# A fused two-block kernel on one core: the first norm by column halves, gate units as two matmuls per k tile, channel sums on VectorE, a masked quarter left out, and one convolution tile on GpSimd

## The reference, cut to what matters

```python
def _even_layer(x, norm_g, w_in, b_glu, w_dw, b_dw, ln_g, ln_b, w_pw, b_pw, w_out):
    z = _rmsnorm(x, norm_g) @ w_in                       # 2048 -> 7 x 1024
    a_val, a_gt, a_gate, q, k, v, b_gate = _split_cols(z, [1024] * 7)
    ya = _conformer_conv(a_val + b_glu[:1024], a_gt + b_glu[1024:],
                         w_dw, b_dw, ln_g, ln_b, w_pw, b_pw) * jax.nn.silu(a_gate)
    ...                                                  # causal attention of 8 heads on q, k, v: yb
    ...                                                  # yb * silu(b_gate), and both through w_out

def _conformer_conv(a_val, a_gt, w_dw, b_dw, ln_g, ln_b, w_pw, b_pw):
    u = a_val * jax.nn.sigmoid(a_gt)
    y = lax.conv_general_dilated(u, w_dw[:, None, :], window_strides=(1,), padding=[(30, 0)],
                                 feature_group_count=1024) + b_dw     # 31 taps per channel
    y = jax.nn.silu(_layernorm(y, ln_g, ln_b))                        # over the 1024 channels
    return y @ w_pw + b_pw
```

## Time and profile before

| | us |
|---|---|
| three runs: median (lowest to highest) | 2568.4 (2568.16 to 2569.23) |
| the profiled execution | 2565.47 |
| its span, first to last instruction | 2563.7 |
| PE busy | 2486.2 (97%) |
| DVE busy | 1622.7 (63%) |
| ACT busy | 1176.6 (46%) |
| POOL busy | 151.1 (6%) |

### The profile page before, as it was taken

The page is one execution under the profiler, slowest core; times in us unless marked ns, Lnnn a source line. Parts: engine busy times, 40 slices in busy tenths (PEclk is TensorE's granted clock), DMA queues, the critical chain, the costliest instruction groups (busy, mean ns, idle before and its releaser), DMA issues.

```text
span 2563.7 us, 35901 instructions
## 1 busy us (share of the span) xinstructions
PE 2486.2 (97%) x14366; PEld 2175.2 (85%) x14366; DVE 1622.7 (63%) x1941; ACT 1176.6 (46%) x1371; POOL 151.1 (6%) x136
## 2 busy tenths in 40 slices
PE   6999999999889999999999999999999999999998
PEld 6888998898778788988888888888888888888886
DVE  4799755545674776486565545445677557755764
ACT  5433754444464554542345444334655334433333
POOL 0000000000200100000000000000022001210220
PEclk9999999999999999999999999999999999999999
DMA  7565436554424555554026555535455555655553
GB/s 236 165 197 189 142 131 229 150 165 133 144 83 159 157 185 172 170 164 132 1 82 214 187 180 192 164 132 184 160 182 196 192 183 183 196 187 185 186 174 138
DMA packets 341284, 422.91 MB, mean 165 GB/s; under 512 B 14491, under 2 KB 267178, under 8 KB 340394
## 3 DMA queue, kind: packets, MB, share of 16 engines
q1 hardware_dynamic: 338620, 411.66, 49.1%
q0 software_dynamic: 2160, 8.40, 1.0%
q10 hardware_dynamic: 382, 1.11, 0.1%
HBM read 419.05 MB, written 2.10 MB: 164 GB/s over the span
## 4 chain that ended last, share of the span: by engine, by line
PE 94%; DVE 4%; ACT 2%; issue 0%; DMA 0%; ACTq 0%; DVEq 0%
PE ps L678 29%; PE ps L679 15%; PE ps L723 9%; PE ps L725 9%; PE ps L724 9%; PE ps L681 4%; PE ps L682 4%; PE ps L683 4%; PE ps L944 3%; PE ps L754 1%; DVE w_lo L1844 1%; PE ps L912 1%; PE ps L885 1%; PE ps L1141 1%; PE ps L1132 1%; PE ps L901 0%
## 5 line engine op out<-in xcount | busy, mean ns | idle before, releaser
L678 PE MATMUL ps<-h_cat,w_hi 128*128 128x512 f32 x3200 | 1137.0, 400 | 8.2 <-DVE qo L1877 8.0
L679 PE MATMUL ps<-h_cat,w_lo 128*128 128x256 f32 x3200 | 897.7, 281 | 0.0
L1844 DVE TENSOR_TENSOR w_lo<-ring,w_hi 128x2048 fp32r<-128x2048 f32 (+2 forms) x282 | 592.3, 2102 | 278.6 <-ACT w_hi L1221 275.6
L678 PEld LDWEIGHTS ps<-h_cat,w_hi 128*128 128x128 f32 x3200 | 602.2, 188 | 159.1 <-DVE w_lo L1844 6.1
L679 PEld LDWEIGHTS ps<-h_cat,w_lo 128*128 128x128 f32 x3200 | 605.5, 189 | 2.1 <-issue 1.9
L1221 ACT ACTIVATE w_hi<-ring 128x2048 fp32r<-128x2048 f32 (+2 forms) x282 | 495.8, 1759 | 98.9 <-PE ps L725 84.5
L1840 DVE TENSOR_TENSOR w_lo<-ring,w_hi 128x2048 fp32r<-128x2048 f32 (+1 forms) x136 | 303.1, 2232 | 232.0 <-ACT w_hi L1218 231.9
L1218 ACT ACTIVATE w_hi<-ring 128x2048 fp32r<-128x2048 f32 (+1 forms) x136 | 252.7, 1862 | 285.4 <-PE ps L725 263.4
L723 PE MATMUL ps<-w_hi,h_cat 128*128 128x512 f32 x704 | 275.9, 392 | 4.7 <-DVE h_cat L2013 3.0
L725 PE MATMUL ps<-w_hi,h_cat 128*128 128x512 f32 x704 | 274.7, 390 | 0.0
L724 PE MATMUL ps<-w_lo,h_cat 128*128 128x512 f32 x704 | 274.7, 390 | 0.0
(11 more groups left out here) (380 smaller groups left out, 2460.0 us busy)
## 6 DMA issues: line engine op xcount, KB each, us to landing
ring<-in_w_ffn_up SPq DMA_DIRECT2D x44, 2048.0 KB, 8.0
ring<-in_even_w_in SPq DMA_DIRECT2D x28, 2048.0 KB, 8.1
ring<-in_w_mix_in SPq DMA_DIRECT2D x28, 2048.0 KB, 8.3
ring<-in_w_ffn_down SPq DMA_DIRECT2D x16, 2048.0 KB, 8.0
ring<-in_odd_w_in SPq DMA_DIRECT2D x11, 2048.0 KB, 8.3
ring<-in_even_w_out SPq DMA_DIRECT2D x8, 2048.0 KB, 8.1
ring<-in_odd_w_out SPq DMA_DIRECT2D x8, 2048.0 KB, 8.1
ring<-in_w_mix_out SPq DMA_DIRECT2D x8, 2048.0 KB, 8.1
```

What stands on the lines that cost most here:

```text
L678: mm(o[:, 0:2 * T], whi[slot][:, k, :], flat(cat[:, k]), start=first, stop=False)
L679: ins = mm(o[:, T:2 * T], wlo[slot][:, k, :], cat[:, k, 0, :], start=False, stop=end)
L1844: tt(wlo[slot][:, 0:g.kt, 0:m], chunk(c % RING, g)[:, :, u0:u0 + m], whi[slot][:, 0:g.kt, 0:m].bitcast(F32), ALU.subtract).then_inc(sem["l ...
```

## The change

Five things change, with the orders that follow from them.

1. First norm. x comes in four transfers (two token halves by two column halves), each with its own semaphore; ACT squares four quarters; the row of the norm's gain comes first and is turned and copied by itself; POOL loads the other eleven rows and makes `w_hi` of unit 0 in two casts; DVE makes its `w_lo` in two halves between pieces of `h_cat`.
2. Gate units. The segments e_gt, e_bgate, e_agate, o_gate0, o_gate1 and g_z (48 units) become paired: ACT copies, DVE adds, and a further ACT instruction applies sigmoid or silu in place (`gate_function`), with a new semaphore `gated`.
3. Channel sums. DVE sums 8 tiles into one (`channel_sum`), and PE multiplies that one by ones, at u = 10 and u = 12. The centring on DVE moves from step 14 to step 13.
4. Masked quarter. Scores of the first 128 queries against the last 128 keys are not made, nor the transpose of that quarter; DVE clears that part of banks 2 and 3 once, at the start of e_bgate.
5. Tile 0 of the convolution goes to POOL as 31 multiplies and 31 adds of 128x256. DVE keeps 217 taps, in groups of tiles (1, 2), (3, 4), (5, 6, 7): 6 or 7 per unit from e_val's sixth on, 7 in e_v, and 8, 8, 8, 7 in e_bgate.

```diff
+        self.gated = name in ("e_gt", "e_bgate", "e_agate", "o_gate0", "o_gate1", "g_z")
-        self.paired = staged or name in ("e_k", "e_q", "o_iq", "o_q", "g_c", "x_q", "x_k")
+        self.paired = staged or self.gated or name in ("e_k", "e_q", "o_iq", "o_q", "g_c", "x_q", "x_k")
...
     @block.sync
-        sp.dma_start(x[:, 0, :], a["x"][0, 0:P]).then_inc(sem["x_loaded0"], 16)
+        for h in range(2):
+            cols = slice(h * D // 2, (h + 1) * D // 2)
+            sp.dma_start(x[:, 0, cols], a["x"][0, 0:P, cols]).then_inc(sem[f"x_loaded0{h}"], 16)
...
     GpSimd
+        for row in first_table[1:]:
+            load_rows(pool, row, "params_loaded")
+        pool.wait_ge(sem["first_loaded"], 16)
+        for half in range(2):
+            k = slice(8 * half, 8 * half + 8)
+            pool.tensor_copy(whi[0][:, k, :], chunk(0, order[0])[:, k, 0:P]).then_inc(sem["first_hi"], 1)
...
+        pool.wait_ge(sem["params_ready"], 3)
+        pool.wait_ge(sem["posted"], S["e_val"].s0 + 1)
+        for tap in range(TAPS):
+            w = prm[:, COL["dw"] + tap * CT:COL["dw"] + tap * CT + 1]
+            if tap:
+                pool.wait_ge(sem["pool_tap"], 2 * tap)
+            pool.tensor_tensor(xsq[:], u[:, 0, tap:tap + T], w.to_broadcast([P, T]), ALU.mult).then_inc(sem["pool_tap"], 1)
+            pool.wait_ge(sem["pool_tap"], 2 * tap + 1)
+            before = conv[:, 0, :] if tap else prm[:, COL["b_dw"]:COL["b_dw"] + 1].to_broadcast([P, T])
+            pool.tensor_tensor(conv[:, 0, :], xsq[:], before, ALU.add).then_inc(sem["pool_tap"], 1)
...
     @block.tensor: e_scores, the transposes, beside e_bgate and e_agate
             for qt in range(TT):
-                ins = mm(o[:, qt * T:(qt + 1) * T], qe[:, h, qt * P:(qt + 1) * P], ke[:, h, :], start=True, stop=True)
+                keys = (qt + 1) * P
+                ins = mm(o[:, qt * T:qt * T + keys], qe[:, h, qt * P:(qt + 1) * P], ke[:, h, 0:keys], start=True, stop=True)
...
-                for qt in range(TT):
+                for qt in range(kt, TT):
...
                 if u_ == 1:
-                    pe.wait_ge(sem["emptied"], 4)
+                    pe.wait_ge(sem["quarter_clear"], 1)
...
-                if u_ == 11:
-                    pe.wait_ge(sem["conv_tap"], TAPS * CT)
+                if u_ == 10:
+                    pe.wait_ge(sem["conv_total"], 1)
+                    pe.wait_ge(sem["masked"], HEADS - 1)
+                    mm(ps[2][:, 0:T], ones[:], xsq[:], start=True, stop=True).then_inc(sem["conv_mean"], 1)
+                if u_ == 12:
+                    pe.wait_ge(sem["conv_total"], 2)
                     pe.wait_ge(sem["masked"], HEADS)
-                    for c in range(CT):
-                        ins = mm(ps[2][:, 0:T], ones[:], conv[:, c, :], start=(c == 0), stop=(c == CT - 1))
-                    ins.then_inc(sem["conv_mean"], 1)
...
+                    mm(ps[3][:, 0:T], ones[:], xsq[:], start=True, stop=True).then_inc(sem["conv_var"], 1)
...
     @block.scalar: drain
-            if g.staged:
+            if g.gated:
+                if g.name == "e_bgate":
+                    act.wait_ge(sem["pool_tap"], 2 * TAPS)
+                    if j >= 1:
+                        act.wait_ge(sem["conv_tap"], taps_through(j))
+                ins = af(gated_tile(g, jj), src, ACT.Copy)
+            elif g.staged:
...
+        def gate_function(g, j, i=None):
+            jj = j if i is None else j + 4 * i
+            act.wait_ge(sem["summed"], g.d0 + jj + 1)
+            v = gated_tile(g, jj)
+            if g.name == "e_gt":
+                ins = af(v, v, ACT.Sigmoid, bias=col("b_glu", CT + jj))
+            else:
+                ins = af(v, v, ACT.Silu)
+            ins.then_inc(sem["gated"], 1)
...
     @block.vector
+        def channel_sum(tiles):
+            nc.vector.tensor_reduce(xsq[:], tiles[:].rearrange("p c t -> p t c"), AX_X, ALU.add).then_inc(sem["conv_total"], 1)
...
-            taps = conv_taps(204, 11)
+            taps = conv_taps(186, 8)
...
+                if u_ == 0:
+                    dve.wait_ge(sem["emptied"], 4)
+                    for bank_ in (2, 3):
+                        ins = nc.vector.memset(ps[bank_][:, P:T], 0.0)
+                    ins.then_inc(sem["quarter_clear"], 1)
                 if u_ < 4:
                     taps(0, b)
+                if u_ == 9:
+                    dve.wait_ge(sem["conv_tap"], len(TAP_ORDER))
+                    dve.wait_ge(sem["pool_tap"], 2 * TAPS)
+                    channel_sum(conv)
...
                 if u_ == 14:
+                    dve.wait_ge(sem["conv_sq"], 1)
+                    channel_sum(csq)
+                if u_ == 13:
                     dve.wait_ge(sem["conv_mean"], 1)
...
     key_beside (o_gate0)
+            if 4 * i + b == 3:
                 dve.wait_ge(sem["cq_std"], 1)
                 ch.link(nc.vector.reciprocal(orq[:], orq[:]))
```

## The result

| | us |
|---|---|
| before, median of five runs (lowest to highest) | 2568.16 (2566.41 to 2569.23) |
| changed, median of five runs | 2580.38 (2576.16 to 2581.55) |
| ratio, 95% interval | 1.0048 (1.0037 to 1.0059) |
| span of the profiled execution, before and changed | 2563.7 and 2576.7 |

The changed kernel is slower by 12.2 us. 2577 was forecast for the likeliest case, with a range of 2555 to 2588.

A forecast was written before the change was run, and what follows sets the result against it. PE was taken as the bound (busy 97%, 94% of the chain). Removed -20.5, added +11.4 and POOL's tile +18 sum to +8.9 us; on the median 2568.4 that gave 2577, range 2555 to 2588.

The forecast's parts named there:

- A: Convolution stretch: POOL alternates with VectorE's taps, each holding the other up; +18, total 2577; chance 0.49.
- B: Convolution stretch: VectorE's trains of taps keep POOL out, which finishes late; +12, total 2571; chance 0.13.
- C: Convolution stretch: little contention between POOL and VectorE, 0 to 2; total 2559.3, faster; chance 0.28.
- D: Added waits at e_bgate's entrance and the heads at their low ends, POOL near 0; total 2551; chance 0.10.
- E: First norm: unit 0 starts no earlier, so its -6.5 is 0; no chance of its own.
- POOL's term: From e_val on: POOL's 62 instructions and VectorE's taps block each other; +18, from 12 to 29.
- First norm: Start of the kernel: PE's 6.02 idle before unit 0 goes, first matmul earlier; -6.5, ends -4 and -9.
- Gate units: 48 gate units: two matmuls instead of three save 0.11 each; -5.3, ends -4 and -7.
- Channel sums: L826 and L831: PE sums one tile instead of eight, -6.05; VectorE's strided sum beside the heads, +1.9.
- Masked quarter: Scores of 8 heads: half of two score instructions and one transpose go, 0.33 per head; -2.6.
- the loop beside the heads: ACT and DVE loop grows from 7.05 to 7.47 and becomes the bound; +0.2 for each of about eight units.
- Entrance to e_bgate: Start of e_bgate: clearing delays `w_lo`, +0.8; bank freed late by VectorE's sum, +5.0; together +5.8, ends +2 and +8.

The follow-up runs named there:

- pool_out: The changed kernel with POOL's 62 convolution instructions left out, tile 0 cleared and not computed: 2560.62 us, ratio 0.9971.
- pool_memset: The changed kernel with POOL's 62 instructions replaced by 62 memsets that only write, tile 0 not computed: 2561.84 us, ratio 0.9978.
- tile_alone: The kernel before with only POOL's tile of the convolution and the new dealing of the taps: 2584.00 us, ratio 1.0065.
- pe_sums: The changed kernel with the channel sums on PE again and the centring in step 14: 2577.31 us, ratio 1.0035.
- clear_later: The changed kernel with VectorE's clearing and its wait for e_v's last copy one step later in e_bgate: 2571.41 us, ratio 1.0017.
- tile_on_dve: The changed kernel with tile 0 back on VectorE and the taps dealt out as before the change: 2567.64 us, ratio 1.0001.
- bgate_plain: The changed kernel with e_bgate alone as plain units again, three matmuls and ACT's drain with silu: 2576.34 us, ratio 1.0033.
- after_again: The changed kernel, unedited, run once more for a second profile: 2582.13 us, one run.

## Why the prediction was right, and where it was not

*The mechanism.* The forecast was A, POOL's instructions between VectorE's taps. Its rows in a stage far away held for another form and another place. pool_out, pool_memset and tile_alone show it. B (trains shut POOL out) falls, since POOL had a turn behind nearly every tap and was done by 140.5; C falls with the 17.3, D with the 5.3 that PE waits at e_bgate's entrance, and E with the first matmul at 17.62.

*POOL's term: +18 forecast, +17.3 measured.* That the two are so close is in part luck. An instruction cost VectorE 0.38 and not 0.5, and by the working's own line for 0.35 that gives not much over 12. Against that, PE's unit took 5.55 and not 5.65, and POOL had nine turns a unit, not ten, with ten of the 62 free instead of 12: 9 x 0.38 + 5.8 - 5.55 is 3.67 a unit, 52 turns last 5.8 units, and less 4.6 of slack that is about 16.6, an estimate. Three of these units have six taps instead of seven, which takes off 1.2. Measured, the unit behind the last wait starts at 138.77 against 123.12 in pool_out, 15.7 late. That is VectorE's lag, which the working named. The unit ends 17.3 late, and the 1.6 between the two are its slow clock, a term that the working did not have. So PE's waiting, which the prediction put at about 18, was 11.0: the slow units fill a part of the lag.

*First norm: -6.5 forecast.* The first matmul came 6.4 earlier, e_gt's second drain 6.0.

*Gate units: -5.3 forecast, 0.11 each.* e_gt's units took 5.55 (from 45.84 to 51.39) and not the 5.65 forecast, 0.21 less than before, and o_gate1 and g_z gained 1.4 each. With e_gt paired, e_val to e_q ran at 5.55 too: without POOL (pool_out) the stretch from e_gt's last drain to e_q's takes 133.1 against 135.7 before. The forecast had nothing for these 2.6; the last section says what is known of them. o_gate0 lost 0.7: PE waited 1.9 for a `gate` sum, where 1.6 was forecast.

*Channel sums: -6.05, and +1.9 beside the heads.* This is the term that was mis-sized most: 2.3 was taken for the sum on VectorE, from a subtraction of as many elements.

```profile
320.36 3.75 DVE L2177 TENSOR_REDUCE xsq<-conv 128x256 f32<-128x2048 f32 x1
...
326.27 0.69 PE L844 MATMUL ps<-ident,pe_p 128*128 128x128 f32 x3 [3.12 <-DVE pe_p L2172]
```

The strided sum takes 3.75 (its upper end was 4.6), stands in front of a mask, and PE waits 3.12 for the transposes behind it; the unit behind that wait began at 1.2 GHz. By pe_sums the net gain in this stage was 1.75 in place of 4.15.

*Masked quarter and the loop beside the heads.* Scores take 0.65 instead of 0.86. ACT's splits come 7.40 apart, against a forecast of 7.47 and 7.05 before:

```profile
301.10 1.90 ACT L1264 ACTIVATE w_hi<-ring 128x2048 fp32r<-128x2048 f32 x1
...
308.50 1.90 ACT L1264 ACTIVATE w_hi<-ring 128x2048 fp32r<-128x2048 f32 x1
```

*Entrance to e_bgate: +5.8 forecast.* The size was about right (0.7 and 4.6 of waiting, 1.4 of slow clock; 4.7 came back in clear_later), the cause was not. The prediction put 5.0 to the sum's place and 0.8 to the clearing. clear_later shows that the sum at that place is in time once VectorE may run ahead. The working had taken VectorE to arrive with PE. It arrived 12.7 earlier, and the clearing threw that away; in tile_on_dve, with eight taps a step as before the change, it still arrived 11.0 earlier. The trace of before shows this lead. VectorE's rows at the same place:

```profile
241.73 2.29 DVE L1844 TENSOR_TENSOR w_lo<-ring,w_hi 128x2048 fp32r<-128x2048 f32 x1
243.94 4.44 DVE L2055 SCALAR_TENSOR_TENSOR conv<-u,prm,conv 128x256 f32<-128x256 f32 x11
```

The first is the `w_lo` of e_bgate's first unit. It ends at 244.0, and ACT's last copy of e_v ends only at 255.2: a wait for that copy, put between the two rows, would cost VectorE 11. The row at 257.05, from which the working starts, belongs to the third step of e_bgate.

*The sum.* Forecast +8.9, measured +13.0 in span and +12.2 in the medians. By stages of the profiled executions, the terms gave -7.4 up to e_gt's last drain and it was -7.3. They gave +18 up to e_q's and it was +14.6: 17.3 for POOL, less the 2.6 of the faster units. They gave -1.1 from e_v to e_pw and it was +3.9. They gave -0.5 behind that and it was +1.9, nearly all of it in g_qkv, whose 24 units took 5.55 before and 5.65 in the changed kernel (127.6 and 130.0 from its first drain to its last). So the step that failed is the stage from e_v to e_pw, 5.0 off; the two other differences, -3.4 and +2.4, largely cancel. Of the 5.0, the channel sums make 2.4 and the entrance, by its waits and its slow clock, 0.9. The rest is not located.

## What to carry to other kernels

Before work is given to GpSimd beside a full VectorE, see whether both read SBUF, and take the price from a place in the trace where they already meet: here VectorE was busy for 44.55 of 45.00 us without POOL (pool_out, 85 to 130), and 52 small instructions at 0.38, an estimate of some 20 us, cost it more than the 31 taps that they replaced (12.7). A wait added to an engine that runs ahead costs that engine the lead that it has there (12.7 here, of which the kernel lost about 5), so look for how early it arrives, and see whether the thing waited for is needed at all. When TensorE waits for another engine again and again, count the time by that engine's period; a slower TensorE clock behind a wait adds to it only where TensorE is the bound again.

## What was not expected of the hardware

*Two pitches.* A paired unit took 5.55 in some segments and 5.65 in others, for the same instructions at a granted clock of 1.00. Two executions of the kernel before show it at the same units of g_qkv. ACT's drains in the first, and then in the second:

```profile
892.51 0.38 ACT L1235 ACTIVATE stage<-ps 128x256 f32<-128x256 f32 x1 [3.35 <-PE ps L679]
898.06 0.39 ACT L1235 ACTIVATE stage<-ps 128x256 f32<-128x256 f32 x1 [3.36 <-PE ps L679]
```

```profile
891.41 0.38 ACT L1235 ACTIVATE stage<-ps 128x256 f32<-128x256 f32 x1 [3.46 <-PE ps L679]
897.08 0.38 ACT L1235 ACTIVATE stage<-ps 128x256 f32<-128x256 f32 x1 [3.48 <-PE ps L679]
```

They are 5.55 apart in the one and 5.67 in the other. In the changed kernel e_q's units took 5.55 in the first profile and 5.65 in the second. So the program alone does not set it. But it is not free of the program either: in e_gt and up to the first wait it was 5.55 in all eleven profiles with e_gt paired, and 5.65 in e_val in the three with e_gt plain; behind a wait it was either. In a segment of 24 to 30 units it makes 2.4 to 3 us, which is a good part of the spread of the runs here and why a difference of 3 us between two medians, as of pe_sums and the changed kernel, decides nothing. What sets it stays open.

*Clock behind short waits.* In the changed kernel's first profile PE's next unit ran in part at 1.2 GHz behind waits of 1.88, 2.60, 3.12, 3.35 and 4.59, and at 1.00 behind 1.28 and 1.86. The other profiles show that the length of the wait does not decide it. Behind the second wait of the stretch, 2.61, the unit stayed at a granted clock of 1.00 in pe_sums and bgate_plain. Behind the wait of 3.12 for the transposes it stayed there in after_again, and behind one of 1.84 in the same profile it fell. What decides stays open.
